# Hyena input projection: the low parts of the weights on VectorE instead of GpSimd, and modulation slabs summed in halves

## The reference, cut to what matters

```
def dwconv3(u, w, b):
    up = jnp.pad(u, ((0, 0), (1, 1), (0, 0)))
    return up[:, :-2] * w[0] + up[:, 1:-1] * w[1] + up[:, 2:] * w[2] + b
...
def hyena_mixer(h, w_in, conv_w, conv_b, filt, d_skip, w_out):
    u = dwconv3(h @ w_in, conv_w, conv_b)
    x0, x1, v = jnp.split(u, 3, axis=-1)
    v = v * x1
...
    m = jax.nn.silu(cond) @ w + b        # ada_params_2: six modulation vectors of a layer
```

## Time and profile before

| what | value |
|---|---|
| median of 3 runs | 3809.65 us (3809.39 to 3812.03) |
| profiled execution, its own time | 3807.93 us |
| its span, first to last instruction | 3806.0 us |
| mean granted TensorE clock | 0.932 |
| busy share of the span: TensorE, VectorE, ScalarE, GpSimd | 88%, 48%, 30%, 11% |
| the stage that is changed, in the span | about 899 us to 1063 us |

### The profile page before, as it was taken

One profiled execution on the slowest core, in us unless ns is written; L12 is line 12 of the kernel. 1 busy time (PEld: TensorE's weight loads), 2 busy tenths in 40 slices (PEclk: granted clock), 3 DMA queues, 4 the chain that ended last, 5 costly groups with the idle time before them and its releaser, 6 DMA issues. The chain is left out here.

```text
span 3806.0 us, 47649 instructions
## 1 busy us (share of the span) xinstructions
PE 3340.8 (88%) x18241; PEld 2257.7 (59%) x18241; DVE 1824.8 (48%) x2900; ACT 1131.5 (30%) x1882; POOL 428.9 (11%) x428
## 2 busy tenths in 40 slices
PE   8999899899988899977999998699886996998886
PEld 6767587766755787746888886344332773433332
DVE  6774687457874877354565564311112543111112
ACT  3042443234213332345445443111111321111111
POOL 1200000001300000012233230111110000111110
PEclk7999999999989999988999998799998997999998
DMA  6340355322612355211121120699997204999995
GB/s 226 130 148 23 102 177 181 133 100 89 243 67 66 122 178 187 68 27 32 32 58 37 32 76 2 261 405 400 425 411 284 108 24 201 415 406 407 401 391 206
DMA packets 224678, 692.89 MB, mean 182 GB/s; under 512 B 28019, under 2 KB 108115, under 8 KB 199284
## 3 DMA queue, kind: packets, MB, share of 16 engines
q1 hardware_dynamic: 194016, 652.63, 45.0%
q10 hardware_dynamic: 11764, 20.97, 1.5%
q0 software_dynamic: 18720, 16.84, 1.3%
HBM read 700.78 MB, written 40.94 MB: 195 GB/s over the span
## 5 line engine op out<-in xcount | busy, mean ns | idle before, releaser
L642 PE MATMUL psum<-work_rounded 128*128 128x512 f32 (+1 forms) x2224 | 811.6, 405 | 76.9 <-DVE work_rounded L636 32.7
L642 PE MATMUL psum<-work_rounded,ring_rounded 128*128 128x512 f32 (+1 forms) x1824 | 726.9, 399 | 0.0
L642 PEld LDWEIGHTS psum<-work_rounded 128*128 128x128 f32 x2224 | 429.2, 193 | 189.6 <-issue 78.7
L3678 PE MATMUL psum<-ring,fixed 128*64 128x512 f32 x1184 | 414.7, 658 | 96.3 <-DMA ring<-in_w 55.0
L631 ACT ACTIVATE work_rounded<-ring 128x1024 fp32r<-128x1024 f32 x204 | 214.3, 1057 | 804.5 <-PE psum L642 665.5
L642 PE MATMUL psum<-fixed_rounded,work_rounded 128*128 128x512 f32 (+1 forms) x1088 | 435.6, 400 | 0.0
L642 PEld LDWEIGHTS psum<-work_rounded,ring_rounded 128*128 128x128 f32 x1824 | 353.2, 194 | 81.1
L3833 DVE TENSOR_TENSOR work<-work,psum 64x512 f32<-64x512 f32 (+1 forms) x64 | 44.2, 691 | 700.0 <-ACT work L3763 546.1
L636 DVE TENSOR_TENSOR ring_rounded<-ring,work_rounded 128x1024 fp32r<-128x1024 f32 x189 | 230.3, 1222 | 274.5 <-ACT work_rounded L631 274.5
L3678 PEld LDWEIGHTS psum<-ring,fixed 128*64 128x64 f32 x1184 | 130.9, 150 | 332.8 <-issue 332.8
L365 DVE SCALAR_TENSOR_TENSOR work<-ring,fixed,work 128x512 f32<-128x512 f32 x364 | 300.6, 835 | 25.5 <-issue 1.7
(11 more groups left out here) (408 smaller groups left out, 5022.2 us busy)
## 6 DMA issues: line engine op xcount, KB each, us to landing
ring<-in_w SPq DMA_DIRECT2D x128, 2048.0 KB, 17.1
work<-in_w SPq DMA_DIRECT2D x64, 2048.0 KB, 21.5
ring<-in_mod_w SPq DMA_DIRECT2D x24, 2048.0 KB, 8.4
ring<-in_ada_w SPq DMA_DIRECT2D x24, 2048.0 KB, 8.1
ring<-in_ffn_w_in SPq DMA_DIRECT2D x44, 1024.0 KB, 7.6
ring<-in_ffn_w_out SPq DMA_DIRECT2D x10, 2048.0 KB, 7.8
ring<-in_w_in_a SPq DMA_DIRECT2D x32, 512.0 KB, 6.6
ring<-in_hy_w_in SPq DMA_DIRECT2D x6, 2048.0 KB, 8.2
```

The lines of the kernel that those rows point to most:

```text
L642: ins = pe.matmul(out, c.rounded(w), c.rounded(x), start=(start and i == 0), stop=(stop and i == 2))
L3678: ins = pe.matmul(c.ps[64 * j:64 * j + 64, 2, :], self.gt_sb[:, k, 0:64], weights(o, j)[:, k, :], start=(k == 0), stop=(k == KD - 1))
```

## The change

`HyenaIn.gpsimd` is taken away. VectorE makes the low part of tile 1 in the norm ahead (`second_low`), and that of tile j + 2 at the head of iteration j of its loop, ahead of the wait for tile j's centre tap. `vector_slab` gets a range of rows k: slab s is now summed in two pieces, rows 0 to 3 behind the convolution of tile 2s - 1 and rows 4 to 7 behind the convolution of tile 2s, and it is given free at the end of the second. The waits of a slab (its arrival, a free accumulator) stand ahead of the first piece. Slab 0 and all other stages keep the whole sum.

```diff
-    def vector_slab(self, dve, s):
+    def vector_slab(self, dve, s, rows=range(KD)):
...
-        for k in range(1, KD):
+        for k in rows:
+            if k == 0:
+                continue
             dve.drain()
             for cond, acc in pairs:
                 ins = dve.scalar_tensor_tensor(out=acc, in0=w[:, k, :], scalar=c.par(cond, k), in1=acc,
                                                op0=ALU.mult, op1=ALU.add)
                 if k == KD - 1:
                     ins.then_inc(self.summed, 1)
-        c.used(dve.drain(), self.n[s])
+        if rows[-1] == KD - 1:
+            c.used(dve.drain(), self.n[s])
...
     def second_low(self, dve):
-        pass
+        self.parts.make_low(dve, 1, self.unit(1))
...
-    def gpsimd(self, pool):
-        for j in range(1, 24):
-            self.parts.make_low(pool, j, self.unit(j))
-
     def vector(self, dve):
         c = self.c
         self.side.vector_slab(dve, 0)
         for j, m in enumerate(self.order):
+            if j + 2 < 24:
+                self.parts.make_low(dve, j + 2, self.unit(j + 2))
             dve.wait_ge(self.centre, self.centre0 + j + 1)
...
-            if j % 2 == 1 and j < 22:
-                self.side.vector_slab(dve, j // 2 + 1)
+            if 1 <= j < 23:
+                self.side.vector_slab(dve, (j + 1) // 2, range(0, 4) if j % 2 else range(4, KD))
         self.side.finish(dve)
```

More of the change, by code:

```diff
@@ L348, in own @@
         return self.c.view(self.acc + 512 * (n % 4), 512)
-    def vector_slab(self, dve, s):
+    def vector_slab(self, dve, s, rows=range(KD)):
         c = self.c
         w = c.slot(self.n[s], KD, 512)
-        c.arrived(dve, self.n[s])
         q = self.before(s)
[L355 to L361, removed]
-        for k in range(1, KD):
+        pairs = [(cond, self.own(s, i)) for i, (cond, _) in enumerate(self.jobs[s])]
+        if rows[0] == 0:
+            c.arrived(dve, self.n[s])
+            for i in range(len(pairs)):
+                if q + i >= 4 and not self.columns:
+                    dve.wait_ge(self.turned, self.turned0 + q + i - 3)
+            for cond, acc in pairs:
+                dve.tensor_scalar(acc, w[:, 0, :], c.par(cond, 0), None, ALU.mult)
+        for k in rows:
+            if k == 0:
+                continue
             dve.drain()
```

## The result

| what | before | changed |
|---|---|---|
| median of 20 runs (lowest to highest), us | 3809.16 (3800.79 to 3812.38) | 3815.24 (3811.58 to 3821.61) |
| ratio, 95% interval | | 1.0019 (1.0012 to 1.0026) |
| profiled execution, its own time, us | 3807.93 | 3815.15 |
| its span, us | 3806.0 | 3813.3 |
| mean granted TensorE clock | 0.932 | 0.931 |

The change makes the kernel slower: the medians stand 6.1 us apart and the averages 7.1 us, the ratio is 0.19% above 1, and its interval does not reach 1.

What follows compares the result with a forecast made beforehand. Bound: a loop of VectorE freeing a slab, load, high part, low part, TensorE. Stage +5.4 to +6.6 us plus 1.5 allowance made +7.8 on 3807.93, 3815.7; plus 1.7 for the median, 3817.5 us. Range 3811.5 to 3822.5 us.

Steps and rivals of the forecast that it cites:

- no change: Outcome for the whole kernel: median within 0.2% (7.6 us) of before, 3802.0 to 3817.3 us; chance 0.42.
- The bound: HyenaIn stage: VectorE's freeing of slabs 2, 4, 6 and 8 for the next weight loads sets the pace.
- The replay: Stage's load loop stepped through by row durations: 27.0 us between releases plus 0.76 per product; end +5.4 to +6.6 us.
- The norm and tile 2: Tile 1's low part (1.13 us) hides in the norm's 2.87 us idle, price 0; tile 2 starts 0.3 us later.
- The loads: Weight slab loads of 2 MB in the stage's loop, taken as 8.3 us from issue to high part.
- The shorter load of the page: Skill page's 6.8 us estimate for a weight slab load, which would make the sum about 4 us less; not followed.
- the rival of faster loads: Weight loads issued apart take 7.0 us; sum only +3 to +4 us, 3813 us; 15 in 100, with other VectorE speedups.
- The allowance: Added 0 to 2.5 us, taken as 1.5, because VectorE or its load is late over 125 us, before 30.
- The time outside the stage: Sign of being wrong: time outside 880 to 1070 us changes by more than 2 us.
- collisions were what made VectorE late: Rival: without GpSimd collisions slabs free earlier, waits at tiles 16 and 20 (1.3 + 6.5 us) go; 3802 us; 8 in 100.
- The clock at the new waits: TensorE at tiles 12, 16, 20: slow clock left open; if tile 20 isn't slow, TensorE is done 2.6 us sooner.

Runs made afterwards that it cites:

- e3_early_split: Changed kernel with both pieces of each slab one tile earlier, behind tiles 2s-2 and 2s-1; 3801.81 us, 0.9986 of the kernel before.
- e1_low_only: Changed kernel with each slab summed whole behind tile 2s-1, low parts still on VectorE; 3804.12 us, 0.9992 of the kernel before.
- e4_late_whole: Changed kernel with each slab summed whole behind tile 2s, no halves; 3830.87 us, 1.0062 of the kernel before.
- e5_h_ahead: Changed kernel with loads h2 to h5 each issued ahead of the modulation slab that stood before them; 3802.46 us, 0.9990 of the kernel before.
- e8_low_after_taps: Changed kernel with the low part of tile j + 2 behind the taps of tile j on VectorE; 3818.74 us, 1.0042 of the kernel before.
- e7_dummy_gpsimd: Changed kernel plus 22 subtractions on GpSimd that nothing needs; 3833.91 us, 1.0065 of the kernel before.

## Why the prediction was right

The measured 3815.24 us lies in the stated range. The outcome that I had called the likelier one, slower by more than 0.2% (0.50 against 0.42 for "no change"), is neither confirmed nor refuted by a ratio of 1.0019 (1.0012 to 1.0026). By its steps:

- **The bound.** That the stage's pace is set by when VectorE reaches the end of slabs 2, 4, 6 and 8 is shown: the same work one tile earlier gives 13.1 us of stage (e3_early_split), a slab without halves one tile later costs 26.4 us (e1_low_only against e4_late_whole), and the loads alone reordered give 9.1 us (e5_h_ahead).
- **The replay.** Forecast and measured, in us: h2 943.2 and 944.17, h3 971.0 and 971.88, h4 1000.3 and 1001.28, h5 1028.8 and 1029.99; tile 12 981.8 and 982.59, tile 16 1011.1 and 1012.05, tile 20 1039.6 and 1041.56; the end of the stage "near 1070" and 1070.04. The step from one release to the next, 27.0 us and 0.76 for a product, was measured as 27.7, 29.4 and 28.7 us against 27.8, 29.3 and 28.5.
- **The norm and tile 2.** The low part of tile 1 in the norm was hidden: VectorE's wait for TensorE's variance shrank from 2.87 to 1.82 us and was still there. TensorE's first matmul of the stage stands at 899.47 against 899.10, and between kernels with the same code up to there it varies from 897.65 to 900.53. Tile 2 starts 17.3 us behind it, before 17.0: +0.3 us as forecast.
- **The loads.** From issue to the high part h2 to h5 took 8.1, 8.3, 8.3 and 9.1 us, against 8.3 in the replay. The shorter load of the page, "DMA: Bandwidth & Descriptors" of the Trainium skill, does not show in any of them, and the rival of faster loads fell. The one slow load, h5's, is 0.8 us of the 2.0 us by which tile 20 came later than in the replay.
- **The allowance.** Here the size was right and the reason given for it was not, so part of it is luck. The replay gave 1067.7 to 1068.9 us for the stage's end, and 1070.04 were measured, 1.1 to 2.3 us more; I had added 1.5 us because VectorE would fall behind over a longer time. It did not: the issues of h2 to h5 came 1.0, 0.9, 1.0 and 1.2 us later than in the replay, so most of the lateness was there at the first of them and hardly grew. Another 0.8 us came from the load of h5. In all I forecast +7.8 us; the stage grew by 7.4 us, its end moved by 7.75 us, and the profiled executions differ by 7.2 us, the averages by 7.1 us and the medians by 6.1 us.
- **The time outside the stage.** I had put it as a sign of being wrong if this changed by more than 2 us. From the stage's end to the end of the span it changed by 0.45 us in all, but as a sum of two larger parts: 3.2 us less up to 1290 us, of which 2.55 us are the faster transposes, and 2.8 us more behind. I had foreseen neither.
- **The rival "collisions were what made VectorE late"** was priced as one case with 8 in 100 and fell, but half of it is true: with the low parts moved and nothing else, the collisions go, the wait at tile 20 goes, that at tile 16 falls from 1.24 to 0.77 us, and the stage is 4.0 us shorter (e1_low_only). What I treated as one change with one sum is two with opposite signs, -4.0 us and +11.4 us of stage.
- **The clock at the new waits.** I left open whether tiles 12, 16 and 20 would run slow. All three did, at 0.70, 0.50 and 0.69 over about 5.6 us. It cost little, since TensorE waited for VectorE again at the next load's first tile, and behind tile 20 VectorE worked without a wait from 1040.18 us to the stage's end.

What stays open: why the transposes behind the stage found the fast clock after and the slow one before, which is worth 2.5 us there, and what took this gain back further on.

## What to carry to other kernels

When a ring of buffers is shared by two streams, the work that frees a place can stand on the other stream's critical path, even if its own result isn't needed for a long time. Before splitting such work into pieces, look where the last piece ends, not where the first begins. Here halves that ended one tile behind the place of the whole cost 11.4 us of stage; halves that ended at its place, and began a tile ahead of it, gained 1.7 us (157.5 against 159.2 us). A count of an engine's work over the stage prices the early and the late halves alike; replaying one turn of the loop row by row gave every issue time within 1.2 us.

## What was unexpected about the hardware

- The length of a wait alone did not tell the clock behind it. In the changed kernel a wait of 2.21 us was followed by a granted clock of 0.69; in e8_low_after_taps one of 2.40 us by 1.00. The rows by stretch, tile 20 of each kernel (busy us of each engine, clock, DMA share, GB/s), changed kernel first:

```profile
1041.50:1047.00 5.50, 5.45 (x17) 4.38 (x18) 4.98 (x7) 0.93 (x2) 0.00 (x0) 0.69 0.95 357
```
```profile
1044.40:1050.00 5.60, 5.58 (x24) 4.58 (x25) 5.17 (x7) 0.00 (x0) 0.00 (x0) 1.00 1.05 392
```

- A `tensor_scalar` with one input in SBUF is held up by GpSimd as well, where the taps, whose other input is in PSUM, are not: in e7_dummy_gpsimd the first instruction of slab 4 took 1.71 us for 0.48, and before the change that of slab 8 took 2.23 us (timelines of VectorE, in this order):

```profile
970.27 1.71 DVE L361 TENSOR_SCALAR work<-ring,fixed 128x512 f32<-128x512 f32 x1
```
```profile
1011.90 2.23 DVE L361 TENSOR_SCALAR work<-ring,fixed 128x512 f32<-128x512 f32 x1
```
